# Normed transpositions for the first token tiles, and first operands made per contraction tile, in a one-core hybrid encoder kernel

## The chip, the cores and the metric

The kernel runs on one core of one Trainium2 chip. The metric is the device time of one execution in microseconds. Engines are named as in the profile: PE is TensorE, DVE is VectorE, ACT is ScalarE, POOL is GpSimd, SP is the engine that issues most DMAs.

## The reference, cut to what matters

One layer of an encoder over 1088 tokens (1024 of a prompt and 64 new ones) of width 1024. The change sits in its first two lines.

```python
h = rms_norm(x, ln_mix_g)      # x / sqrt(mean(x*x) + eps) * ln_mix_g
proj = h @ w_in                # 1024 -> 5632 columns: u, v_g, q, k, v, gates
...                            # gMLP, windowed attention, gates, w_o
x = x + f                      # f: conv FFN: w_up, depthwise conv, gelu, w_down
y = rms_norm(x, ln_final_g)
```

## The kernel before

**Pairs and products.** All large products have the weights' 128 output channels by 1088 tokens as result, and are made two column blocks of weights at a time, a *pair* p. Tokens are cut in two halves of 544, the 8 contraction tiles of 128 into even and odd ones (4 each, KP = 4). A plain pair (0 and 1 are plain) has 8 products k = 0 to 7, each 4 contraction tiles j of 6 matmuls: the two fp32 operands are each split into a high part and a rest (`w_hi`, `w_lo`, `op_hi`, `op_lo`), three passes by two column blocks of 272. Other pairs have seven products with sums of quadrants as operands.

**Operands.** `hi_f` and `lo_f` hold the normed input in fp32. For pair 0 operand 0 is the first half of the tokens with even contraction tiles (`hi_f3`), operand 1 the first half with odd ones (`hi_f5`), operands 7 and 6 are the second half (`lo_f4`, `hi_f4`). ACT rounds an operand to `op_hi` (L1235), DVE subtracts to get `op_lo` (L1647), each in one instruction of 4 times 544 columns. The same for the weights: ACT L1201, DVE L1608, 512 columns each. DVE then makes sums of operands (L1655, L1693, L1658) for the seven-product pairs, and ACT rounds the first of them, `op_hi3`, which waits for L1655.

**The norm.** There are 9 tiles of tokens n (the last has 64 rows); SPLIT = 4, so tile 4 lies across both halves. SP loads them to `xt`. For each, ACT squares and sums rows (`square_x`, L1242), POOL makes the factors 1/sqrt(mean + eps) (`rstd`, L1082 and L1085), PE transposes eight 128x128 blocks to PSUM (`transpose_x`, L2234), ACT copies them to SBUF (`x_tile`, L1192), PE spreads the factors over partitions by one product (`spread_rstd`, L2243), and DVE multiplies block by gain by factor into the operands (its own `x_tile`, L1600), 8 instructions of 128 columns a tile. The copies `xts` are also stored to DRAM by SP (`store_xt`), for the residual much later.

**Order.** Every engine's program is written out by hand and runs in that order; an engine that waits at a semaphore holds everything behind it. Tiles 0 to 5 are normed ahead of the first product. Tiles 6, 7 and 8 are transposed between contraction tiles of products 0 and 1 (`beside_first(k, j)` on PE, called behind product k, tile j). PSUM: `reg[0]`, `reg[1]`, `reg[2]` of two banks each hold products and `side` (banks 6 and 7) everything else.

Of the kernel before, what the change touches and what calls it, by code (L numbers as in the profile page):

```python
# [7 lines left out]
ALU = mybir.AluOpType  # L8
# [127 lines left out]

PAIR_TICKS = 4 * NPROD
# [53 lines left out]
OP_ORDER = [[(n, "w") for n in (0, 1, 7, 6, 3, 2, 5, 4)]]  # L191
# [9 lines left out]
PART = {"w": slice(0, KP), "a": slice(0, KP - 1), "b": slice(KP - 1, KP)}  # L201
# [69 lines left out]
def program(nc, x_prompt, x_sample, cache_k, cache_v, cache_conv, ln_mix_g, w_in, ln_v_g, ln_v_b, w_s, b_s,  # L271
# [3 lines left out]
    with ExitStack() as ctx:  # L275
# [15 lines left out]
        def put(reg, name, shape, dt=F32, at=0):  # L291
# [119 lines left out]

        bank = [ps[:, i] for i in range(4)]
# [20 lines left out]
        s_tab = sem("s_tab")  # L433
# [227 lines left out]
        def _(sp):  # L661

            def load_x(n):
                if n >= XT:
                    sp.wait_ge(s_xt_p, n - XT + 1)
                    sp.wait_ge(s_sq, n - XT + 1)
                sp.dma_start(xt[0:rows_of(n), n % XT, :], token_rows(n)).then_inc(s_x_in[n % XT], 16)

# [12 lines left out]
            for n in range(NT):  # L681
# [386 lines left out]
        def _(pool):  # L1068
# [9 lines left out]
            def rstd(n, table, sums, factors):  # L1078
# [6 lines left out]
                pool.tensor_tensor(table[0:r, 2, n:n + 1], table[0:r, 1, n:n + 1], half_neg[0:r, :],  # L1085
                                   ALU.pow).then_inc(s_rstd, 1)

            for n in range(NT):
                rstd(n, stat, 0, 0)

            def distances():
                pool.wait_ge(s_hf, NT + 1)
# [1487 lines left out]
```

## Time and profile before

| | |
|---|---|
| time, median of 3 runs | 1651.01 us (1650.73 to 1655.04) |
| the profiled execution's own time | 1649.72 us |
| its span | 1647.9 us |
| mean granted TensorE clock | 0.994 of full |
| PE busy | 1614.5 us, 98% of the span |
| DVE, ACT, POOL busy | 1152.0, 706.7, 71.7 us |
| instructions | 32421 |

The profile is of one execution. Its span is the part between the first and the last instruction; its own time is 1.8 us longer. Busy time is counted from instructions' starts and ends, matmul ends are modelled, and starts of successive matmuls tell the pace better than their durations do.

### The profile page before, as it was taken

What the parts mean: (1) busy time and instruction counts of PE and PEld (TensorE: products, weight loads), DVE (VectorE), ACT (ScalarE), POOL (GpSimd) and SP (SyncE); (2) the same over time, 40 slices, a digit from 0 to 9 for tenths busy, and PEclk for the clock granted to TensorE, in tenths of its full rate; (3) what the DMA queues carried; (4) which work ended last, traced back from release to release, by engine and by line L of the source; (5) the groups of instructions that cost most, each with busy time, mean ns of one, the idle gap of its engine ahead of it and who ended that gap; (6) DMA issues with size and microseconds to landing.
All of it is one profiled execution on the core that took longest, in us unless ns stands there. A gap on an engine that the chain in (4) does not pass through costs nothing. (4 is left out here: it accounts for less than half of the span.)

```text
span 1647.9 us, 32421 instructions
## 1 busy us (share of the span) xinstructions
PE 1614.5 (98%) x12886; PEld 1574.7 (96%) x12886; DVE 1152.0 (70%) x2078; ACT 706.7 (43%) x1292; POOL 71.7 (4%) x141
## 2 busy tenths in 40 slices
PE   6999999999999999999999999999999999999998
PEld 6999999999999999999999999999999999999997
DVE  6566565656658868696525888888888776767566
ACT  7344444444444336364434534444333334343312
POOL 2000000000000000001112100000000000000001
PEclk8999999999999999999999999999999999999999
DMA  7444434343437864757743233333333427363122
GB/s 248 151 150 118 133 107 137 102 138 100 119 111 204 242 215 161 246 161 169 166 135 99 59 115 97 107 106 106 106 106 107 131 72 266 120 241 105 69 78 110
DMA packets 272472, 227.03 MB, mean 138 GB/s; under 512 B 43335, under 2 KB 223363, under 8 KB 272323
## 3 DMA queue, kind: packets, MB, share of 16 engines
q1 hardware_dynamic: 138750, 154.36, 28.2%
q10 hardware_dynamic: 131269, 66.15, 14.3%
q0 software_dynamic: 2304, 4.46, 1.7%
q8 instruction: 103, 1.69, 0.4%
q14 instruction: 46, 0.38, 0.1%
HBM read 150.56 MB, written 74.36 MB: 136 GB/s over the span
## 5 line engine op out<-in xcount | busy, mean ns | idle before, releaser
L2296 PE MATMUL ps<-op_hi,w_hi 128*128 128x272 f32 x3672 | 775.6, 292 | 15.5 <-issue 5.6
L2296 PE MATMUL ps<-op_hi,w_lo 128*128 128x272 f32 x3672 | 760.6, 289 | 0.0
L2296 PE MATMUL ps<-op_lo,w_hi 128*128 128x272 f32 x3672 | 758.6, 288 | 0.0
L2296 PEld LDWEIGHTS ps<-op_hi,w_hi 128*128 128x128 f32 x3672 | 576.1, 189 | 32.7 <-issue 30.2
L2296 PEld LDWEIGHTS ps<-op_lo,w_hi 128*128 128x128 f32 x3672 | 578.0, 189 | 0.0
L2296 PEld LDWEIGHTS ps<-op_hi,w_lo 128*128 128x128 f32 x3672 | 575.0, 189 | 0.0
L1608 DVE TENSOR_TENSOR w_lo<-raw,w_hi 128x512 fp32r<-128x512 f32 x256 | 173.7, 698 | 157.2 <-ACT w_hi L1201 157.2
L1201 ACT ACTIVATE w_hi<-raw 128x512 fp32r<-128x512 f32 x256 | 153.7, 625 | 134.1 <-PE ps L2296 90.1
L1280 ACT ACTIVATE u<-ps 128x544 f32<-128x544 f32 x106 | 66.2, 624 | 237.6 <-PE ps L2296 237.4
L1201 ACT ACTIVATE w_hi<-w_f 128x512 fp32r<-128x512 f32 x159 | 95.3, 625 | 39.6 <-DVE w_f L1628 30.4
L1608 DVE TENSOR_TENSOR w_lo<-w_f,w_hi 128x512 fp32r<-128x512 f32 x159 | 104.8, 683 | 3.9 <-ACT w_hi L1201 3.4
L1305 ACT ACTIVATE sc_sb<-sc_sb,att_stat 128x192 f32<-128x192 f32 (+2 forms) x136 | 59.1, 435 | 92.6 <-DVE att_stat L1874 92.5
L1647 DVE TENSOR_TENSOR op_lo<-lo_f,op_hi 128x2176 fp32r<-128x2176 f32 (+2 forms) x32 | 75.1, 2348 | 21.9 <-ACT op_hi L1235 21.8
L1235 ACT ACTIVATE op_hi<-lo_f 128x2176 fp32r<-128x2176 f32 (+2 forms) x32 | 62.1, 1959 | 48.2 <-DMA lo_f<-g_spill 28.3
L1753 DVE TENSOR_TENSOR quad<-u,ps 128x544 f32<-128x544 f32 x69 | 49.3, 715 | 31.0 <-ACT u L1280 19.6
L1280 ACT ACTIVATE m1c<-ps 128x544 f32<-128x544 f32 x53 | 32.6, 615 | 59.3 <-PE ps L2296 41.7
L1647 DVE TENSOR_TENSOR op_lo<-r,op_hi 128x2176 fp32r<-128x2176 f32 (+2 forms) x25 | 42.8, 1723 | 14.9 <-ACT op_hi L1235 14.7
L1968 DVE SCALAR_TENSOR_TENSOR conv<-a_ext,conv_w,conv 128x1090 f32<-128x1090 f32 x22 | 29.8, 1354 | 29.0 <-ACT conv L1428 29.0
L1428 ACT ACTIVATE conv<-a_ext,consts,conv_w 128x1090 f32<-128x1090 f32 x22 | 28.6, 1301 | 46.7 <-issue 40.7
L1753 DVE TENSOR_TENSOR quad<-m1c,ps 128x544 f32<-128x544 f32 x23 | 16.6, 720 | 45.3 <-PE ps L2296 44.5
L1868 DVE CUSTOM_DVE_ANT_0 sc_sb<-ps,bias,sinks 128x192 f32<-128x192 f32 (+2 forms) x136 | 47.1, 401 | 0.3 <-issue 0.3
L1433 ACT ACTIVATE conv<-conv 128x1090 f32<-128x1090 f32 x22 | 24.6, 1117 | 49.2 <-DVE conv L1973 49.2
(191 smaller groups left out, 1514.1 us busy)
## 6 DMA issues: line engine op xcount, KB each, us to landing
in_spill<-quad SPq DMA_DIRECT2D x88, 272.0 KB, 2.3
raw<-in_w_up_dram ACTq DMA_DIRECT2D x44, 512.0 KB, 4.7
raw<-in_w_in_dram ACTq DMA_DIRECT2D x42, 512.0 KB, 5.4
g_spill<-value_out SPq DMA_DIRECT2D x22, 544.0 KB, 2.7
t_spill<-t_buf SPq DMA_DIRECT2D x8, 1088.0 KB, 4.3
lo_f<-g_spill SPq DMA_DIRECT2D x8, 1088.0 KB, 7.9
lo_f<-t_spill SPq DMA_DIRECT2D x8, 1088.0 KB, 9.3
raw<-in_w_down_dram ACTq DMA_DIRECT2D x16, 512.0 KB, 5.2
```

Of the source, the lines that this page charges most:

```text
L1201: act.activation(w_hi[n][:], weight_source(p, n), copy).then_inc(s_w_hi, 1)
L1235: act.activation(op_hi[at][:, j], operand_source(g, n)[:, j], copy).then_inc(s_op_hi, 1)
L1280: act.activation(two((m1c, u2, u3)[i][:]), reg[0][:, :, 0:HB], copy).then_inc(s_copied, 1)
L1305: act.activation(x, x, ACT.Exp, bias=a[:, 1, e:e + 1], accum_out=a[:, 3, e:e + 1])
L1428: act.activation(conv[:, 2:EXT], a_ext[:, 2:EXT], ACT.Identity, bias=b_conv_c[:, f:f + 1], scale=conv_w[:, 2, f:f + 1]).then_inc(s_c0, 1)
L1433: act.activation(conv[:, 2:EXT], conv[:, 2:EXT], ACT.Gelu_apprx_tanh).then_inc(s_gelu, 1)
L1608: dve.tensor_tensor(w_lo[n][:], weight_source(p, n), w_hi[n][:].bitcast(F32), ALU.subtract).then_inc(s_w, 1)
L1647: dve.tensor_tensor(op_lo[at][:, j], operand_source(g, n)[:, j], op_hi[at][:, j].bitcast(F32), ALU.subtract).then_inc(s_op, 1)
L1753: dve.tensor_tensor(two(out), two(first[:]), reg[region][:, :, 0:HB], op).then_inc(s_comb, 1)
L1868: last = dve.tensor_tensor_reduce(sc_sb[:, i % 2, h, columns_of(n, c)], side[:, h, columns_of(n, c)], bias[:, h, seen(n, c):SPAN], HD ** - ...
L1968: dve.scalar_tensor_tensor(cv, a_ext[:, 1:EXT - 1], conv_w[:, 1, f:f + 1], cv, ALU.mult, ALU.add).then_inc(s_c1, 1)
L2296: last = pe.matmul(out[:, h, 0:HB], (w_hi, w_lo)[a][place][:, j, :], (op_hi, op_lo)[b][at][:, j, HB * h:HB * h + HB], start=fresh and j == ...
```

## The change

Tiles 1 to 4 are no longer transposed and then scaled. POOL makes a matrix `diag[n]`, the identity times the tile's factors, and PE multiplies each block of the tile by it, which transposes and norms at once (`turn_normed`, 8 fp32 matmul calls a tile into `side`, even contraction tiles in bank 0, odd ones in bank 1). DVE applies the gains while it copies from PSUM (`x_turned`: one instruction of 4 times 128 columns for the even and one for the odd tiles). The gains come by a small DMA and transposition of their own. Tile 0 keeps the old way but is copied by DVE. Since the store for the residual still needs the plain transposes, tile 1 is also transposed ahead of the first product, and tiles 2, 3 and 4 within products 4, 5 and 6 of pair 0; the other tables follow in product 7. Tiles 5 to 8 keep the old way; 5 is normed beside product 1. Operands 0, 1, 7 and 6 of pair 0 are rounded and subtracted contraction tile by contraction tile (544 columns each), and PE waits for one tile at a time. SP holds the loads of tiles 6 to 8 until the first weights have landed. In the diff below the function `beside_first` shown whole is ACT's; the last lines are of PE's `beside_first`; the wait on `s_xts` for tiles 3 and 4 is in PE's `transpose_x`.

```diff
+TURNED = (0, 1, 5, 6, 7, 8, 2, 3, 4)
+COPIED = (5, 1, 6, 7, 8, 2, 3, 4, "tables")
+DIAG = range(1, SPLIT + 1)
...
-OP_ORDER = [[(n, "w") for n in (0, 1, 7, 6, 3, 2, 5, 4)]]
+OP_ORDER = [[(n, str(k)) for n in (0, 1, 7, 6) for k in range(KP)] + [(n, "w") for n in (3, 2, 5, 4)]]
...
+        turned_at = (reg[0], reg[1], side, side, side, reg[2], reg[2], reg[2], reg[2])
...
             for n in range(5):
                 load_x(n)
             load_weights(sp, 0)
-            for n in range(5, NT):
+            load_x(5)
+
+            sp.wait_ge(s_raw, 32)
+            for n in range(6, NT):
                 load_x(n)
...
+                if turned:
+                    last.then_inc(s_var, 1)
+                    pool.wait_ge(s_var, factors + n + 2)
+                    last = pool.tensor_tensor(diag[n][:], ident[:], table[:, 2, n:n + 1].broadcast_to([P, P]), ALU.mult)
...
-            square_x(0)
-            x_tile(0)
-            square_x(1)
...
-            for n in range(2, 6):
+            for n in range(6):
                 square_x(n)
-                x_tile(n)
             weight_hi(0, 0)
             weight_hi(0, 4)
-            operand_hi(0, 0, "w")
-            operand_hi(0, 1, "w")
+            for k in range(KP):
+                operand_hi(0, 0, str(k))
+            x_tile(5)
+            x_tile(1)
...
+            def beside_first(k, j):
+
+                if (k, j) == (3, 1):
+
+                    act.wait_ge(s_sq, NT)
+                if j == 0 and k in (3, 4):
+                    for i in range(KP):
+                        operand_hi(0, {3: 7, 4: 6}[k], str(i))
+                if (k, j) in ((4, 1), (6, 1), (7, 1)):
+                    x_tile({4: 2, 6: 3, 7: 4}[k])
+                if (k, j) == (7, 2):
+                    tables()
...
+            def x_turned(n, half, k):
+
+                dve.wait_ge(s_rb_p, spread_count(n, k))
...
+                dve.tensor_tensor(place_of(half, k)[:, :, t0:t0 + b - a], side[:, k].rearrange("p (i t) -> p i t", i=KP)[:, :, a:b], gain,
+                                  ALU.mult).then_inc(s_hf, 1)
...
+                if n in (3, 4):
+                    pe.wait_ge(s_xts, COPIED.index(n - 1) + 1)
...
+            def turn_normed(n):
+
+                pe.wait_ge(s_x_in[n], 16)
+                pe.wait_ge(s_rstd, n + 1)
+                for k in range(2):
+                    if n > 1:
+                        pe.wait_ge(s_hf, normed_count(n - 1, 0, k))
+                    for i in range(KP):
+                        kt = 2 * i + k
+                        last = pe.matmul(side[:, k, i * P:i * P + P], xt[:, n, kt * P:kt * P + P], diag[n][:], start=True, stop=True)
+                    last.then_inc(s_rb_p, 1)
...
+                if p == 0 and j:
+                    pe.wait_ge(s_op, op_count(0, operand, str(j)))
...
-                if (k, j) in ((0, 0), (0, 3), (1, 1)):
-                    transpose_x({(0, 0): 6, (0, 3): 7, (1, 1): 8}[k, j])
-                if (k, j) in ((0, 2), (1, 0), (1, 3)):
-                    spread_rstd({(0, 2): 6, (1, 0): 7, (1, 3): 8}[k, j])
+                if (k, j) in ((1, 0), (1, 2), (3, 0), (3, 2)):
+                    spread_rstd({(1, 0): 5, (1, 2): 6, (3, 0): 7, (3, 2): 8}[k, j])
+                if (k, j) in ((1, 0), (2, 1), (3, 0), (4, 2), (5, 2), (6, 2)):
+                    transpose_x({(1, 0): 6, (2, 1): 7, (3, 0): 8, (4, 2): 2, (5, 2): 3, (6, 2): 4}[k, j])
```

Three places show how instructions move. The first is PE's program from its start to the first product (`xt_113` is the input, `stat_110` the factors). Before:

```order
L2234 MATMUL ps<-ident_106,xt_113 128x128 [waits s_x_in1]
L2234 MATMUL ps<-ident_106,xt_113 128x128 x7
L2308 MATMUL ps<-ident_106,tab_rows_123 128x110 [waits s_tab_in]
L2309 MATMUL ps<-ident_106,tab_rows_123 128x54
L2243 MATMUL ps<-ident_106,stat_110 128x128 [waits s_rstd]
L2234 MATMUL ps<-ident_106,xt_113 128x128 [waits s_tab,s_x_in2]
L2234 MATMUL ps<-ident_106,xt_113 128x128 x7
```

With the change, from the spreading of tile 0's factors:

```order
L2332 MATMUL ps<-ident_106,stat_110 128x128 [waits s_rstd]
L2321 MATMUL ps<-ident_106,xt_113 128x128 [waits s_x_in1]
L2321 MATMUL ps<-ident_106,xt_113 128x128 x7
L2344 MATMUL ps<-diag1_126,xt_113 128x128 [waits s_rstd,s_x_in1]
L2344 MATMUL ps<-diag1_126,xt_113 128x128 x7
L2344 MATMUL ps<-diag2_127,xt_113 128x128 [waits s_hf,s_rstd,s_x_in2]
L2344 MATMUL ps<-diag2_127,xt_113 128x128 x3
L2344 MATMUL ps<-diag2_127,xt_113 128x128 [waits s_hf]
L2344 MATMUL ps<-diag2_127,xt_113 128x128 x3
```

Transposes of tiles 2 to 5 with a spreading each gave way to products with the diagonals of tiles 1 to 4, four calls for each parity, and the transposition of tile 5.

The second place is ACT's program from the stores of pair 0's first quadrants to the weights of pair 1 (`quad` is a result, `lo_f3_73` the sum that DVE makes, `xts2_118` the copy of tile 2). Before:

```order
L1379 ACTIVATE quad2_104<-ps 128x544 [waits s_product]
L1235 ACTIVATE op_hi3_52<-lo_f3_73 128x2176 [waits s_op,s_t,s_hf]
L1201 ACTIVATE w_hi0_77<-raw_98 128x512 [waits s_product,s_raw]
L1201 ACTIVATE w_hi4_81<-raw_98 128x512 [waits s_product,s_raw]
L1379 ACTIVATE quad1_103<-ps 128x544 [waits s_product]
```

With the change:

```order
L1421 ACTIVATE quad2_104<-ps 128x544 [waits s_product,s_sq]
L1281 ACTIVATE op_hi6_55<-hi_f4_67 128x544 [waits s_hf] x4
L1281 ACTIVATE op_hi3_52<-lo_f3_73 128x2176 [waits s_op,s_t,s_hf]
L1231 ACTIVATE xts2_118<-ps 128x1024 [waits s_xt_p]
L1247 ACTIVATE w_hi0_77<-raw_98 128x512 [waits s_product,s_raw]
L1231 ACTIVATE xts3_119<-ps 128x1024 [waits s_xt_p]
L1247 ACTIVATE w_hi4_81<-raw_98 128x512 [waits s_product,s_raw]
L1421 ACTIVATE quad1_103<-ps 128x544 [waits s_product]
```

The copies of tiles 2 and 3 are new here, and the copy of tile 2 stands behind `op_hi3`, which waits for the sum (`s_t`).

The third place is PE's program in product 5 of pair 0, from its third contraction tile. Before:

```order
L2296 MATMUL ps<-op_hi2_51,w_hi4_81 128x272 x2
L2296 MATMUL ps<-op_lo2_58,w_hi4_81 128x272 x2
L2296 MATMUL ps<-op_hi2_51,w_lo4_88 128x272 x2
L2296 MATMUL ps<-op_hi2_51,w_hi4_81 128x272 x2
L2296 MATMUL ps<-op_lo2_58,w_hi4_81 128x272 x2
```

With the change:

```order
L2401 MATMUL ps<-op_lo2_58,w_hi4_81 128x272 x2
L2401 MATMUL ps<-op_hi2_51,w_lo4_88 128x272 x2
L2321 MATMUL ps<-ident_106,xt_113 128x128 [waits s_xts,s_x_in3]
L2321 MATMUL ps<-ident_106,xt_113 128x128 x7
L2401 MATMUL ps<-op_hi2_51,w_hi4_81 128x272 [waits s_op]
```

The transposition of tile 3 stands between two contraction tiles, and waits for ACT's copy of tile 2 (`s_xts`), because both use `side`.

## Rows read from the trace of the kernel before

**Rows 1.** The page, part 1: busy us (share of the span) xinstructions

```profile
PE 1614.5 (98%) x12886; PEld 1574.7 (96%) x12886; DVE 1152.0 (70%) x2078; ACT 706.7 (43%) x1292; POOL 71.7 (4%) x141
```

**Rows 2.** Timeline, PE: start us, us, engine line op xcount [idle before <-releaser]

```profile
4.73 3.65 PE L2234 MATMUL ps<-ident,xt 128*128 128x128 f32 x16 [4.73 <-DMA xt<-in_x_prompt_dram]
...
9.56 1.06 PE L2234 MATMUL ps<-ident,xt 128*128 128x128 f32 x8
...
23.79 0.79 PE L2296 MATMUL ps<-op_hi,w_hi 128*128 128x272 f32 x2 [5.09 <-issue]
...
54.68 0.52 PE L2296 MATMUL ps<-op_hi,w_hi 128*128 128x272 f32 x2 [0.34 <-DVE w_lo L1608]
```

**Rows 3.** Windows of the start; the last two numbers are DMA share and GB/s

```profile
0.00:9.00 9.00, 4.14 (x19) 3.61 (x19) 0.00 (x0) 4.49 (x6) 1.69 (x12) 1.00 0.79 296
9.00:12.20 3.20, 2.59 (x21) 2.19 (x20) 2.64 (x11) 3.15 (x7) 1.27 (x4) 1.00 1.15 315
12.20:13.60 1.40, 1.27 (x10) 1.12 (x10) 1.40 (x7) 1.40 (x4) 0.27 (x2) 1.00 1.11 376
...
24.00:28.00 4.00, 4.00 (x19) 4.00 (x20) 4.00 (x7) 1.46 (x3) 2.77 (x2) 0.50 0.01 2
```

**Rows 4.** Timeline of ACT, columns as in rows 2

```profile
4.96 1.06 ACT L1242 ACTIVATE x_junk<-xt 128x1024 f32<-128x1024 f32 x1
5.92 0.19 ACT L1242 ACTIVATION_READ_ACCUMULATOR x_junk<-xt 128x1 f32 x1
...
9.30 1.03 ACT L1192 ACTIVATE xts<-ps 128x1024 f32<-128x1024 f32 x1
...
17.98 1.19 ACT L1201 ACTIVATE w_hi<-raw 128x512 fp32r<-128x512 f32 x2
...
46.71 2.03 ACT L1235 ACTIVATE op_hi<-lo_f 128x2176 fp32r<-128x2176 f32 x1 [4.12 <-DVE lo_f L1655]
48.64 1.13 ACT L1201 ACTIVATE w_hi<-raw 128x512 fp32r<-128x512 f32 x2
```

**Rows 5.** Timeline of POOL

```profile
6.47 0.56 POOL L1085 TENSOR_TENSOR stat<-stat,columns 128x1 f32<-128x1 f32 x1
...
24.78 1.89 POOL L1082 TENSOR_SCALAR stat<-stat 128x1 f32<-128x1 f32 x1 [6.65 <-ACT x_junk L1242]
```

**Rows 6.** Timeline of PE at the mixing of tokens, fp32 products at full clock

```profile
511.34 1.95 PE L2430 MATMUL ps<-ws_t,gs 128*128 128x128 f32 x16
513.04 0.50 PE L2296 MATMUL ps<-op_hi,w_hi 128*128 128x272 f32 x2
```

**Rows 7.** Timeline of DVE

```profile
9.56 9.62 DVE L1600 SCALAR_TENSOR_TENSOR hi_f<-xts,consts,ps 128x128 f32<-128x128 f32 x40 [9.56 <-PE ps L2243]
...
44.21 2.42 DVE L1655 TENSOR_TENSOR lo_f<-lo_f,hi_f 128x2176 f32<-128x2176 f32 x1
...
53.94 1.89 DVE L1608 TENSOR_TENSOR w_lo<-raw,w_hi 128x512 fp32r<-128x512 f32 x3
```

**Rows 8.** Groups by form: busy us, mean ns of one | idle before

```profile
L1120 POOL TENSOR_TENSOR m1c<-m1c,u 128x544 f32<-128x544 f32 x6 | 8.4, 1396 | 43.6 <-ACT u L1411 43.6
...
L1647 DVE TENSOR_TENSOR op_lo<-r,op_hi 128x544 fp32r<-128x544 f32 x8 | 6.5, 808 | 5.4 <-ACT op_hi L1235 5.4
...
L2211 DVE TENSOR_TENSOR xy<-ps,xy 128x512 f32<-128x512 f32 x8 | 5.5, 690 | 3.9 <-PE ps L2547 3.9
```

**Rows 9.** Timeline of PE after its wait at 1400 us

```profile
1403.14 0.49 PE L2296 MATMUL ps<-op_hi,w_hi 128*128 128x272 f32 x2 [2.97 <-DVE xy L1777]
...
1405.47 0.65 PE L2296 MATMUL ps<-op_lo,w_hi 128*128 128x272 f32 x2
1405.92 0.66 PE L2296 MATMUL ps<-op_hi,w_lo 128*128 128x272 f32 x2
...
1407.99 0.41 PE L2296 MATMUL ps<-op_lo,w_hi 128*128 128x272 f32 x2
1408.24 0.41 PE L2296 MATMUL ps<-op_hi,w_lo 128*128 128x272 f32 x2
```

More of the change, by code:

```diff
@@ L133, in chunk, with normed_count, spread_count @@
     return a * P, min(b * P, T)
+TURNED = (0, 1, 5, 6, 7, 8, 2, 3, 4)
+COPIED = (5, 1, 6, 7, 8, 2, 3, 4, "tables")
+NORMED = ("gains", "copy") + tuple((n, int(n > SPLIT), k) for n in range(SPLIT) for k in range(2)) \
+    + ((SPLIT, 0, 0), (SPLIT, 0, 1), (SPLIT, 1, 0), (SPLIT, 1, 1)) + tuple((n, 1, k) for n in range(SPLIT + 1, NT) for k in range(2))
+DIAG = range(1, SPLIT + 1)
+SPREAD = tuple((n, k) for n in range(NT) for k in range(2 if n in DIAG else 1))
+def normed_count(n, half, k):
+    return NORMED.index((n, half, k)) + 1
+def spread_count(n, k=0):
+    return SPREAD.index((n, k)) + 1
 PAIR_TICKS = 4 * NPROD
@@ L410, in program @@
         pset = [ps[:, 0:3], ps[:, 3:6]]
+        turned_at = (reg[0], reg[1], side, side, side, reg[2], reg[2], reg[2], reg[2])
+        factors_at = {n: reg[2][:, 0, 0:P] if n == 0 else side[:, n % 2, 0:P] for n in range(NT) if n not in DIAG}
         bank = [ps[:, i] for i in range(4)]
@@ L432, in program @@
         s_tab_p = sem("s_tab_p")
[L433 removed]
+        s_gain_in = sem("s_gain_in")
         s_x_in = sems("s_x_in", XT)
@@ L1075, in _, with rstd @@
                                pattern=[[-1, P]], channel_multiplier=1).then_inc(s_zero, 1)
-            def rstd(n, table, sums, factors):
+            def rstd(n, table, sums, factors, turned=False):
                 r = rows_of(n)
@@ L1583, in _, with place_of @@
         def _(dve):
[L1585 to L1602 removed]
+            def place_of(half, k):
+                return ((hi_f[3], hi_f[5]), (lo_f[4], hi_f[4]))[half][k]
@@ new lines, in gains, with first_copy, x_tile @@
+            def gains():
+                dve.wait_ge(s_tab_p, 1)
+                dve.tensor_copy(mix_g, reg[2][:, 1, P:P + KT]).then_inc(s_hf, 1)
+            def first_copy():
+                dve.wait_ge(s_xt_p, 1)
+                dve.tensor_copy(xts[0][:], turned_at[0].rearrange("p b (k t) -> p (b k) t", k=4)).then_inc(s_hf, 1)
+            def x_tile(n):
+                r, half = rows_of(n), int(n > SPLIT)
+                if n:
+                    dve.wait_ge(s_xts, COPIED.index(n) + 1)
+                else:
+                    dve.wait_ge(s_hf, NORMED.index("copy") + 1)
+                dve.wait_ge(s_rb_p, spread_count(n))
+                t0 = n * P - half * QT
+                for k in range(2):
+                    for i in range(KP):
+                        last = dve.scalar_tensor_tensor(place_of(half, k)[:, i, t0:t0 + r], xts[n][:, 2 * i + k, 0:r],
+                                                        mix_g[:, 2 * i + k:2 * i + k + 1], factors_at[n][:, 0:r], ALU.mult, ALU.mult)
+                    last.then_inc(s_hf, 1)
```

192 lines of the change are left out of this document (108 added, 84 removed).

## The prediction

> **What bounds the kernel now.** The first part of the page comes first: PE is busy 98% of the span [rows 1]. So the kernel is as long as PE's work plus the times PE stands still, and a change gains only what it takes from either. The timeline of PE shows where it stands still: the first product starts at 23.79, behind 5.09 us of idle time, and pair 1 starts at 54.68 after a wait of only 0.34 us [rows 2]. Of some 33 us in which PE isn't busy (1647.9 less 1614.5) about 20 lie ahead of the first product. The windows show that PE also starts slow: 0.50 of its clock is granted from 24 to 28 us [rows 3].
>
> From pair 1 on PE goes on without a gap to speak of, so I work out when pair 1 starts with the change. The difference to 54.68 is the forecast, as long as nothing behind it depends on the start.
>
> **Up to the first product.** The input comes at DMA speed: 9 us at 296 GB/s are 2.66 MB, which is tiles 0 to 4 (2.62 MB); 3.2 us at 315 bring the first weights (1.05 MB) to about 12.2, and 1.4 at 376 bring tile 5 to 13.6 [rows 3]. ACT now only squares. A square holds it for 1.15 us (4.96 to the end of 5.92 + 0.19), so tile n's sum is there at 6.1 + 1.15n up to tile 4 at 10.7, and tile 5, which waits for its data, at 14.75 [rows 4]. POOL ends a factor 0.9 us after the sum (6.11 to 7.03 for tile 0) [rows 5], and adds the diagonal. No row shows that product. 544 columns of a POOL product take 1.396 us [rows 8]; 128 of them in proportion are 0.33, and 1.4 is the upper bound. I take 0.4, by the proportion and a little for the start. Diagonals 1 to 4 are then there at about 8.7, 10.0, 11.4 and 12.7.
>
> PE transposes tile 0 and then tile 1 at the pace of the 16 transposes of before, 0.228 us each [rows 2], to about 9.1. A turn is 8 fp32 calls, 16 instructions of 128 columns. The mixing of tokens has the same form: 16 of them hold PE for 1.70 us (511.34 to 513.04) at full clock [rows 6]. Four turns are 6.8 us, to 15.9; at half clock they would be 13.6, which is the other bound. I take full clock, because before PE had gone from 0.228 to 1.06 / 8 = 0.13 us a transpose by 9.56 [rows 2], and is busier now. The diagonals are no later than PE. DVE empties a bank of 512 columns in 0.61 to 0.69 [rows 8] while PE fills the other in 0.85, so it keeps up: with its copy of tile 0 and the 8 old instructions (9.62 / 40 = 0.24 each [rows 7]) it is at 9.9 when the first bank is full.
>
> Behind tile 5's square, at 14.75, ACT rounds two weights (1.19 [rows 4]) to 15.9 and the first quarter of the operand to 16.5. DVE makes the last pieces of tile 4 (to 16.25), a weight's rest (1.89 / 3 = 0.6 [rows 7]) and the first quarter of `op_lo`. 544 columns take 0.808 us in the mean [rows 8], while a quarter of the long instruction is 0.6; I take 0.68 from start to start. **The first product starts at 17.6, 6.2 us earlier than before.**
>
> **To product 4.** From there DVE sets the pace. In order: three quarters of operand 0 (2.05), a weight (0.6), the rest of tile 4 (2 times 0.5), a weight (0.6), tile 5 (8 times 0.25 = 2.05), operand 1 (2.7), tile 6 (2.05), a weight (0.6): 29.25. PE has meanwhile done products 0 to 2 at 3.0 us each (two matmuls each 0.25 [rows 9], 24 in a product) with two transpositions, and waits for that last weight. It then does one contraction tile (0.75) and spreads tile 7's factors: 30.2. DVE norms tile 7 to 32.25; tile 8's factors come at 32.4 from PE's place behind tile 2 of product 3, and DVE is done at 34.05; the first quarter of operand 7 follows, and **product 4 starts at 34.8**.
>
> **The stall that the change makes.** Transpositions of tiles 2, 3 and 4 now share `side`, and each waits for ACT's copy of the one ahead. ACT's copy of tile 2 stands behind `op_hi3`, and that waits for DVE's sum of operands, which comes after all quarters of operands 7 and 6. Before, ACT already waited 4.12 us for this sum, but nothing of PE's stood behind it [rows 4]. Now:
> - DVE: 7 more quarters, 4.75, to 39.5, and the sum, 2.42 [rows 7], to 41.95.
> - ACT: `op_hi3` holds it for 1.93 (46.71 to 48.64) and a copy takes 1.03 [rows 4]: 44.95.
> - PE arrives at tile 3's transposition behind 7 contraction tiles (5.25) and tile 2's transposition (8 of 0.106 by rows 6, 0.85) at 40.9.
>
> PE stands still for about 4.1 us, to 45.05. Behind PE's waiting transposition is all of pair 0 that is left: 3 + 0.25 products (9 contraction tiles, 6.75), two transpositions (1.7), the tables (0.25), and 0.2 for the copy of tile 4, which ACT does only after product 6. That is 8.9 us, so pair 1 starts at 54.0 at full clock. DVE's part for pair 1 is ready earlier: its sum begins at 39.5, and the same list took from 44.21 to about 54.6 before [rows 7], so it ends at about 50.
>
> A stall of that length costs clock too. After 2.97 us of idle time at 1400 PE went from 0.25 us for two matmuls to 0.45, and back by 1407.99: about 3.4 us at that pace, 7 or 8 rows that lose 0.2 each, 1.5 us [rows 9]. After the 5.09 us at the start it ran at 0.50 for some 4.8 us and lost about 2.3 [rows 2, 3]. I take 1.9. **Pair 1 starts at 55.9, 1.2 us later than before.**
>
> In the sum: 6.2 us are gained at the first product; pair 0 loses a slow clock of 2.3 at its start, but takes on three transpositions (2.55), a spreading (0.2) and the tables (0.25), stands still some 2.4 us for DVE in products 3 and 4 and 4.1 us for ACT, and loses 1.9 to the clock. The stores of tiles 2 to 4 are late too (tile 4's at about 52). What needs their room or SP's turn behind them comes in the second half of pair 1 or later, and the products of pair 1 (8 of 3.0) hide them, so I cost them at nothing; without that cover PE would wait for the landing, a few us.
>
> The profiled execution would become 1649.7 + 1.2 = 1650.9; it lies 1.3 below the median of the runs, so the median would be **1652.2 us**.
>
> **A rule against the row.** PE's clock had risen after nothing but transposes, as said above. The Trainium skill (TensorE: Matmul & The Clock Gate, Part 4: PE-mode transpose) says that transposes don't count as activity for the clock gate. By that rule the turns would be the first work that counts, and the trace contradicts it for now, since PE's pace doubled behind 16 transposes. What it would do is the third rival below.
>
> POOL's 1.89 us for a 0.19 us kind of instruction at 24.78 [rows 5], beside a long DVE subtraction of two SBUF operands, is a warning for the diagonals, but beside DVE's work with a PSUM operand POOL took 0.56. The Trainium skill (GPSIMD Engine Reference, 8. Key points) has POOL share its SBUF interfaces with DVE when that has two SBUF inputs.
>
> **The rivals.**
> - *The stall without its price in clock.* PE's idle time is broken up or the clock holds: pair 1 at 54.0, 0.7 earlier, 1650.3 us. For it: nothing but that the granted clock falls at moments that a trace can't foretell. Chance 0.2.
> - *No stall.* ACT comes to the copy in time, and PE reaches pair 1 at 54.0 - 4.1 = 49.9, just when DVE has its weights: 4.7 us gained, 1646.3. Against it: the order on ACT is fixed, and the sum can't come before operand 6. Chance 0.08.
> - *Turns begin slow, slower by a front that is late.* If the first two turns run at half clock, everything behind moves by 3.4 us, pair 1 to 59.3: 1655.6. Chance 0.05.
> - *The whole turning is slow.* With all four turns at half clock, or a diagonal of 1.4 us held up by DVE, the first product comes up to 6.8 us later than I say, and the extra work and the stall stay: up to 1659. It decides when the first product starts behind 21.4 (3.8 later), from where the loss passes 5 us. Chance 0.08.
> - *The forecast*: 0.55, from 1650.5 to 1654. The rest, 0.04, for transfers of pairs 1 and 2 that come late.
>
> **The numbers.** 0.3% is 5 us, about what the measurement can tell. The forecast, the first rival and most of the second and third lie within: 0.85. Faster by more needs the second at its upper end and a start better than mine: 0.05. Slower: the last rival and part of the third, 0.10. For 8 times in 10 I take 1647.5 to 1655.5: it leaves out half of the second rival and the fourth.
>
> **What would show it.** The first product at 17 to 18.5 and product 4 at 34 to 36; an idle time of 3 to 5 us ahead of tile 3's transposition in product 5, put down to ACT's copy; a granted clock near 0.5 behind it; ACT idle before `op_hi3` until DVE's sum; pair 1 at 54 to 57. The forecast is wrong if PE isn't idle there, if the turns take over 2.5 us a tile, or if PE gains or loses gaps after pair 1.

## The result: 6 us slower, and the profile after

The change takes 1658.42 us in the median of 7 runs (1657.12 to 1663.4), the kernel before 1651.99 in its 7 (1649.33 to 1655.04): a ratio of 1.0043, interval 1.0032 to 1.0055. Measured once more it had 1658.38 (11 runs) beside 1653.04 (34 runs), ratio 1.0033, 1.0019 to 1.0048. The forecast was 1652.2, with a range of 1647.5 to 1655.5, so it is wrong by 6.2 us.

The page of the change, first part. PE is as busy a share as before [rows 1], but its busy time has grown by 8.3 us, about the length of the turns, which come on top of the transpositions; time at half clock counts as busy too.

```profile
PE 1622.8 (98%) x12943; PEld 1582.7 (96%) x12943; DVE 1151.8 (70%) x2062; ACT 707.6 (43%) x1304; POOL 72.6 (4%) x145
```

The timeline of PE up to pair 1 (start us, us, engine, line, operation, count, [idle before <- releaser]), to be read beside [rows 2]. L2401 are products, L2321 transpositions of x, L2344 turns by a diagonal.

```profile
4.59 1.97 PE L2321 MATMUL ps<-ident,xt 128*128 128x128 f32 x8 [1.32 <-DMA xt<-in_x_prompt_dram]
7.71 0.80 PE L2332 MATMUL ps<-ident,stat 128*128 128x128 f32 x2 [1.15 <-POOL stat L1119]
8.30 1.92 PE L2321 MATMUL ps<-ident,xt 128*128 128x128 f32 x8
10.00 9.32 PE L2344 MATMUL ps<-diag,xt 128*128 128x128 f32 x64
...
20.99 0.49 PE L2401 MATMUL ps<-op_hi,w_hi 128*128 128x272 f32 x2 [0.79 <-DVE w_lo L1681]
...
39.60 0.49 PE L2401 MATMUL ps<-op_hi,w_hi 128*128 128x272 f32 x2 [1.97 <-issue]
...
43.05 1.48 PE L2321 MATMUL ps<-ident,xt 128*128 128x128 f32 x8
...
49.60 1.06 PE L2321 MATMUL ps<-ident,xt 128*128 128x128 f32 x8 [2.08 <-ACT xts L1231]
...
55.05 1.04 PE L2321 MATMUL ps<-ident,xt 128*128 128x128 f32 x8
...
63.59 1.04 PE L2439 MATMUL ps<-ident,ws_raw 128*128 128x128 f32 x8
```

The first product starts at 20.99, which is 2.8 us earlier than before, not 6.2. Product 4 (39.60) waits 1.97 us for operand 7. Tile 3's transposition (49.60) waits 2.08 us for ACT's copy of tile 2, the stall that was foretold at 4.1. The transposition of `ws_raw`, in pair 1, is at 63.59; before it was at 57.78, 3.1 behind the pair's start at 54.68 [rows 2]. So pair 1 starts at about 60.5, 5.8 later than in this profile of before. The second profiles of both, further down, make that 4.4 in the mean.

The windows of PE at four places (busy us, instructions, granted clock, DMA share, GB/s):

```profile
10.00:12.00 2.00, 2.00 (x11) 1.00 1.20 292
14.00:16.00 2.00, 2.00 (x18) 1.00 0.80 166
42.00:44.00 2.00, 2.00 (x11) 0.51 0.00 0
52.00:54.00 2.00, 2.00 (x11) 0.50 0.75 224
```

Between 10 and 12 us PE starts 11 instructions in 2 us, from 14 on 18: its pace doubled in between, at about 13.4, though the column of the granted clock says 1.00 throughout. Behind both waits it says 0.51 and 0.50, the lower of its two levels (1.2 and 2.4 GHz). ACT around the square of tile 5 and around the copy:

```profile
14.59 1.06 ACT L1288 ACTIVATE x_junk<-xt 128x1024 f32<-128x1024 f32 x1 [2.88 <-DMA xt<-in_x_prompt_dram]
...
46.53 2.02 ACT L1281 ACTIVATE op_hi<-lo_f 128x2176 fp32r<-128x2176 f32 x1 [3.45 <-issue]
48.46 1.00 ACT L1231 ACTIVATE xts<-ps 128x1024 f32<-128x1024 f32 x1
```

`op_hi3` (2.02 us) is there ahead of the copy of tile 2 (48.46), in the order that the prediction read from the code. DVE while it takes the turned tiles from PSUM, and before product 4:

```profile
14.43 0.69 DVE L1674 TENSOR_TENSOR hi_f<-ps,consts 128x512 f32<-128x512 f32 x1 [0.20 <-PE ps L2344]
15.48 0.69 DVE L1674 TENSOR_TENSOR hi_f<-ps,consts 128x512 f32<-128x512 f32 x1 [0.36 <-PE ps L2344]
...
34.08 1.12 DVE L1664 SCALAR_TENSOR_TENSOR lo_f<-xts,consts,ps 128x128 f32<-128x128 f32 x4 [1.40 <-PE ps L2332]
...
37.20 0.86 DVE L1664 SCALAR_TENSOR_TENSOR lo_f<-xts,consts,ps 128x64 f32<-128x64 f32 x4 [0.96 <-PE ps L2332]
...
38.78 2.63 DVE L1720 TENSOR_TENSOR op_lo<-lo_f,op_hi 128x544 fp32r<-128x544 f32 x4
```

Each half of a turned tile takes 1.0 us from start to start, of which DVE works 0.69 and then waits for PE. Later it waits 1.40 and 0.96 us for PE's spreading of tiles 7 and 8 (L2332); operand 7's quarters start at 38.78 and product 4 follows 0.82 us behind. POOL's diagonal and one of its slow instructions:

```profile
8.97 0.40 POOL L1123 TENSOR_TENSOR diag<-ident,stat 128x128 f32<-128x128 f32 x1
...
28.66 1.41 POOL L1116 TENSOR_SCALAR stat<-stat 128x1 f32<-128x1 f32 x1 [3.05 <-ACT x_junk L1288]
```

### The profile page after: what moved, and what is told of

Read it like the earlier page. It is cut to its first block, busy times and chain, and to the rows that moved or that the text cites. A ratio compares the mean times of both kernels' runs of the same rounds, so it can differ in the third digit from the quotient of the medians.

```text
span 1656.6 us, 32537 instructions
## 1 busy us (share of the span) xinstructions
PE 1622.8 (98%) x12943; PEld 1582.7 (96%) x12943; DVE 1151.8 (70%) x2062; ACT 707.6 (43%) x1304; POOL 72.6 (4%) x145
## 4 chain that ended last, share of the span: by engine, by line
PE 61%; issue 11%; DVE 4%; DMA 3%; ACT 1%; POOL 1%; ACTq 0%; POOLq 0%; DVEq 0%; SPq 0%
PE ps L2401 52%; PE ps L2623 3%; DMA lo_f<-g_spill 1%; PE ps L2660 1%; PE ps L2543 1%; DVE op_lo L1720 1%; PE ps L2485 1%; DMA r<-m_spill 1%; DMA r<-o_spill 1%; DMA raw<-in_w_down_dram 1%; POOL r L1173 1%; DVE w_lo L1681 1%; PE ps L2515 1%; PE ps L2533 0%; PE ps L2520 0%
## 5 line engine op out<-in xcount | busy, mean ns | idle before, releaser
L2401 PE MATMUL ps<-op_hi,w_hi 128*128 128x272 f32 x3672 | 775.6, 292 | 15.1 <-DVE xy L1860 4.0
L2401 PE MATMUL ps<-op_hi,w_lo 128*128 128x272 f32 x3672 | 760.7, 289 | 0.0
L2401 PE MATMUL ps<-op_lo,w_hi 128*128 128x272 f32 x3672 | 758.6, 288 | 0.0
L2401 PEld LDWEIGHTS ps<-op_hi,w_hi 128*128 128x128 f32 x3672 | 575.6, 188 | 33.0 <-issue 29.3
L2401 PEld LDWEIGHTS ps<-op_lo,w_hi 128*128 128x128 f32 x3672 | 577.9, 189 | 0.0
L2401 PEld LDWEIGHTS ps<-op_hi,w_lo 128*128 128x128 f32 x3672 | 574.9, 189 | 0.0
L1281 ACT ACTIVATE op_hi<-r 128x2176 fp32r<-128x2176 f32 (+2 forms) x25 | 35.6, 1434 | 21.8 <-PE ps L2401 13.6
```

The costliest lines, as they stand in the source:

```text
L1281: act.activation(op_hi[at][:, j], operand_source(g, n)[:, j], copy).then_inc(s_op_hi, 1)
L2401: last = pe.matmul(out[:, h, 0:HB], (w_hi, w_lo)[a][place][:, j, :], (op_hi, op_lo)[b][at][:, j, HB * h:HB * h + HB], start=fresh and j == ...
```

## The experiments

The table has the places that the experiments speak of: starts on PE in us in one profiled execution each (in brackets the idle time before), the first product, product 4, tile 3's transposition and the `ws_raw` transposition (3.1 behind pair 1's start). "Rest" is from there to the first product that waits for `d_lo`, near 1560. The last columns are the median of the runs and the ratio to the kernel before, measured beside it on the same chip, with its interval; the kernel before had 1652.41 there beside e1, e2, e6 and e7, 1652.66 beside e4, e5 and e8, and 1653.04 beside the rest.

| kernel | product 0 | product 4 | tile 3 | ws_raw | rest | median | ratio |
|---|---|---|---|---|---|---|---|
| before | 23.79 | | | 57.78 | 1500.6 | 1651.99 | |
| before, second profile | 25.13 | | | 59.62 | 1500.4 | 1652.66 | |
| change | 20.99 | 39.60 (1.97) | 49.60 (2.08) | 63.59 | 1503.2 | 1658.42 | 1.0043 |
| change, second profile | 19.89 | 38.51 (1.99) | 48.51 (2.23) | 62.52 | 1505.6 | 1658.38 | 1.0033 [1.0019, 1.0048] |
| e1 copy ahead | 20.99 | 39.59 (1.97) | 47.36 (0) | 59.79 | 1504.1 | 1656.42 | 1.0026 [1.0014, 1.0038] |
| e2 late spread | 19.53 | 38.12 (1.96) | 48.11 (2.03) | 60.56 | 1503.0 | 1659.77 | 1.0043 [1.0027, 1.006] |
| e6 early spreads | 19.74 | 36.81 (0.71) | 46.80 (3.62) | 60.77 | 1507.3 | 1659.03 | 1.0037 [1.0025, 1.0049] |
| e5 filler | 21.34 | 39.95 (1.98) | 49.95 (filled) | 62.41 | 1504.6 | 1657.8 | 1.0028 [1.0017, 1.0039] |
| e4 parts only | 21.38 | | | 57.39 | 1502.3 | 1652.57 | 1.0 [0.9991, 1.0009] |
| e7 all three | 19.47 | 36.53 (0.69) | 42.75 (0) | 55.62 | 1502.4 | 1651.8 | 0.9999 [0.9988, 1.0011] |
| e7 again | 19.16 | 37.07 (1.54) | 43.27 (0) | 56.16 | 1502.2 | 1652.41 | 1.0002 [0.9989, 1.0014] |
| e8 four banks | 20.39 | 37.45 (0.69) | 43.66 (0) | 56.55 | 1511.1 | 1653.7 | 1.0009 [0.9997, 1.002] |
| e9 warm | 18.50 | 36.28 (1.41) | 42.49 (0) | 55.37 | 1504.6 | 1651.93 | 0.9991 [0.9977, 1.0004] |
| e3 one block | 19.37 | 37.31 (1.59) | 42.76 (0) | 55.63 | 1506.9 | 1651.59 | 0.9993 [0.9981, 1.0006] |

**e1: the copy of tile 2 ahead of `op_hi3` on ACT.**

```diff
-                if (k, j) in ((4, 1), (6, 1), (7, 1)):
+                if (k, j) in ((4, 0), (6, 1), (7, 1)):
                     x_tile({4: 2, 6: 3, 7: 4}[k])
```

> The change with ACT's copy of tile 2 moved ahead of its rounding of op_hi3. Theory (PE stands still at tile 3's transposition because that copy stands behind op_hi3): the 2.1 us wait there and the 1.4 us of slow clock behind it go, pair 1 starts at 57.0 instead of 60.5, about 1655 us. Rival (the loss is PE's added work, and the wait hides other lateness): another wait takes its place, at most 0.5 us gained, about 1658 us.

```profile
47.36 1.04 PE L2321 MATMUL ps<-ident,xt 128*128 128x128 f32 x8
...
51.24 1.04 PE L2321 MATMUL ps<-ident,xt 128*128 128x128 f32 x8
```

The stall at tile 3 is gone, and the slow clock behind it: tiles 3 and 4 are 3.88 us apart, in the change 5.45. Product 4's wait is untouched. Pair 1 starts 3.8 us earlier, of which 2.2 is the wait and 1.6 the clock. The median is 2.0 below the change, less than the trace gives.

**e2: the spreading of tile 0's factors behind the transposition of tile 1.**

```diff
             transpose_x(0)
-            spread_rstd(0)
             transpose_x(1)
+            spread_rstd(0)
```

> The change with tile 0's factors spread behind tile 1's transposition instead of ahead of it, so that PE transposes two tiles without a pause. Theory (the first turn ran at half pace because PE paused 1.15 us before its clock had risen): the first turn takes 1.7 instead of 3.4 us, the first product starts at about 18.7 instead of 21.0, about 1656 us. Rival (transpositions don't raise the clock, only the turns do): the turn stays slow, the first product starts at 20.3 or later, about 1658 us.

```profile
4.52 3.67 PE L2321 MATMUL ps<-ident,xt 128*128 128x128 f32 x16 [1.18 <-DMA xt<-in_x_prompt_dram]
...
9.83 8.04 PE L2344 MATMUL ps<-diag,xt 128*128 128x128 f32 x64 [1.02 <-POOL diag L1123]
...
48.11 1.07 PE L2321 MATMUL ps<-ident,xt 128*128 128x128 f32 x8 [2.03 <-ACT xts L1231]
...
52.01 1.04 PE L2321 MATMUL ps<-ident,xt 128*128 128x128 f32 x8
```

The wait of 1.15 us inside the transpositions is gone, and the turns begin at 9.83 at full pace: 7.87 us from there to tile 5's transposition, where the change took 9.16 and its second profile 8.38. The first product comes at 19.53, between the two expected. That the pause had made the turn slow is not shown: with the same edit the turns took 8.00 and 7.95 in e7 but 9.21 in e8, in part at half pace, and without it 8.18 in e6. Behind the same 2.03 us of wait at tile 3 the clock did not fall this time (tile 4's transposition follows by 3.90 us, as in e1). The median does not show the gain of 3 us in pair 1's start; its interval is wide, and the profile is of the shortest of the seven runs (1655.22).

**e6: the spreadings of tiles 7 and 8 earlier on PE.**

```diff
-                if (k, j) in ((1, 0), (1, 2), (3, 0), (3, 2)):
+                if (k, j) in ((1, 0), (1, 2), (2, 3), (3, 0)):
```

> The change with the spreads of tiles 7 and 8 one place earlier on PE, behind (2, 3) and (3, 0). Theory (DVE sets the pace up to product 4 and the sum, and stood still 1.4 and 1.0 us for these two spreads): product 4 starts at 37.2 instead of 39.6, DVE's sum 2.4 us earlier, pair 1 at 58.1, about 1656 us. Rival (PE's own work sets the pace): under 0.5 us gained, 1658 us.

```profile
36.81 0.49 PE L2401 MATMUL ps<-op_hi,w_hi 128*128 128x272 f32 x2 [0.71 <-issue]
...
46.80 1.06 PE L2321 MATMUL ps<-ident,xt 128*128 128x128 f32 x8 [3.62 <-ACT xts L1231]
```

From the first product to product 4 it is 17.07 us, in the change 18.61: DVE's waits for the spreadings were 1.5 us of product 4's lateness. ACT's stall at tile 3 grows to 3.62 us, since PE comes sooner to it, and the slow clock stays behind it (tile 4 follows by 5.44 us). Counted from the first product pair 1 starts 1.6 us earlier, not 2.4, and the median, 1659.03, shows no gain.

**e7: all three edits.**

> The three edits together. Theory: the first product at 18.7, no wait ahead of product 4 and tile 3's transposition, full clock through pair 0, pair 1 at about 50.5, that is 1648.5 us, 3.5 below the kernel before. Rival (the added fp32 products and transpositions cost more than the earlier start is worth): pair 1 no earlier than 54.7, 1652 us or more.

> The kernel with all three edits once more, beside the change itself in the same call. Theory (what follows pair 1 costs the same but for steps of 0.5 to 3 us at later waits that differ from one execution to the next): the first product at 19.5 when PE's pace has doubled by 10 us, and near 21 when it doubles at 13 to 14; a median 6 us below the change and within 1.5 us of the kernel before. Rival (it is faster than before by the 3 us that pair 1 starts earlier): a median of 1649.5.

```profile
36.53 0.49 PE L2401 MATMUL ps<-op_hi,w_hi 128*128 128x272 f32 x2 [0.69 <-issue]
...
42.75 1.04 PE L2321 MATMUL ps<-ident,xt 128*128 128x128 f32 x8
...
47.05 1.06 PE L2321 MATMUL ps<-ident,xt 128*128 128x128 f32 x8 [0.26 <-ACT xts L1231]
```

From the first product to `ws_raw` it takes 36.15 and 37.00 us, in the change 42.60 and 42.63. Pair 1 starts 2.2 us earlier than in the shorter profile of before, but in neither measurement does the median leave that of the kernel before. So these waits and the slow clock behind them are about the change's loss, and without them it is a draw, not the gain of some 3 us that I expected.

**e5: transpositions of the identity while PE waits for ACT.**

```diff
+                if (k, j) == (5, 2):
+                    pe.wait_ge(s_comb, comb_count(0, Q21))
+                    for i in range(18):
+                        pe.transpose(reg[1][:, i % 2, 0:P], ident[:], ident[:])
```

> The changed kernel with 18 transpositions of the identity in the 2.1 us in which PE stood still ahead of tile 3's transposition, so that PE stays busy and its wait for ACT stays. Theory (the standstill lowers the clock, also one of 2 us): the products behind tile 3 run at 0.25 us for two, not at 0.45 for 3.1 us, and pair 1 starts 1.4 us earlier, near 59.1; the median 1.4 below the change. Rival (transpositions count as idle for the clock): the clock drops there as before or earlier, pair 1 at 60.5 or later. A clock that stays with no gain of time would say that the end of pair 0 waits for DVE or ACT.

```profile
47.76 2.13 PE L2433 MATMUL ps<-ident 128*128 128x128 f32 x18
49.95 1.07 PE L2321 MATMUL ps<-ident,xt 128*128 128x128 f32 x8
...
53.87 1.04 PE L2321 MATMUL ps<-ident,xt 128*128 128x128 f32 x8
```

The clock stays: tile 4 follows tile 3 by 3.92 us, where the two profiles of the change have 5.45 and 5.47. So the slow clock behind the stall is worth 1.5 us, apart from the stall. Counted from the first product pair 1 starts 1.5 earlier; the median, 1657.8, is 0.6 below the change and not 1.4. That the filler held the clock is likely but rests on one profile, since the clock also held behind 2.03 us of idle time in e2. The rule weighed in the prediction (the Trainium skill, TensorE: Matmul & The Clock Gate, Part 4: PE-mode transpose) fits neither this nor e9 and the second profile of before, where PE's pace doubled among the first 16 transpositions of x (2.60 and 3.31 us for them, against 3.65 at half pace), with nothing but transpositions ahead.

**e4: operands by contraction tile alone, in the kernel before.** The edit is that of `OP_ORDER`, `PART`, the loops over `operand_hi` and `operand_lo` of operands 0, 1, 7 and 6, and PE's wait for one contraction tile; the norm stays as it was.

> The kernel before with one part of the change alone: operands 0, 1, 7 and 6 of the first generation are made and waited for by contraction tile, the turning stays as it was. Theory (the parts are worth something only until DVE, whose work is the same, ends it): the first product waits for a quarter of op_hi0 and a quarter of op_lo0, so it starts near 20.6 instead of 23.79, product 4 near 38.9, and pair 1 at 53.8 instead of 54.68; median 0.9 us below the kernel before. Rival (the parts are all of what the first products need, and PE runs through): pair 1 at 51.5 and a median 3 us below. Other rival (hidden): pair 1 within 0.3 of 54.7 and the same time.

```profile
21.38 0.79 PE L2303 MATMUL ps<-op_hi,w_hi 128*128 128x272 f32 x2 [2.19 <-DVE w_lo L1610]
```

The first product comes at 21.38, 2.4 us before the earlier of the two profiles of before and 0.4 to 1.5 behind the change. The parts alone thus bring most of what the change gains there. But pair 1 comes at 54.3, 0.4 us before the earlier profile of before, and the time is that of before. Between the two PE now waits 1.6 us for tile 6's factors and 0.7 for ACT, where before it waited 0.3. That fits a pair 0 whose end is set by the lists of the other engines; it wasn't tested apart.

**e8: four banks for the turns, on top of e7.**

```diff
+        turn_at = lambda n: reg[0] if n % 2 else side
...
-                    if n > 1:
-                        pe.wait_ge(s_hf, normed_count(n - 1, 0, k))
+                    if n > 2:
+                        pe.wait_ge(s_hf, normed_count(n - 2, 0, k))
+                    elif n == 1:
+                        pe.wait_ge(s_hf, NORMED.index("copy") + 1)
...
-                        last = pe.matmul(side[:, k, i * P:i * P + P], xt[:, n, kt * P:kt * P + P], diag[n][:], start=True, stop=True)
+                        last = pe.matmul(turn_at(n)[:, k, i * P:i * P + P], xt[:, n, kt * P:kt * P + P], diag[n][:], start=True, stop=True)
```

DVE's `x_turned` reads from `turn_at(n)` too.

> The kernel with all three edits (copy of tile 2 ahead, spread of tile 0 behind tile 1, early spreads) and the products with the diagonal of tiles 1 and 3 in the two banks of reg[0], those of tiles 2 and 4 in side, so that each waits for DVE's reading of two tiles before and not of the one before. Theory A (the 2.0 us a tile are a handshake over two banks between PE and DVE): the 64 instructions take 6.8 to 7.0 us and not 8.2, the first product starts at 18.3 and not 19.5, pair 1 near 51.4, and the median is 1.2 below that of all three edits. Theory B (PE itself takes 0.122 us for one of these at full clock, 2.0 a tile): 8.1 us, first product at 19.4, and the same median as with all three edits.

DVE, with PE at its full pace:

```profile
14.30 0.69 DVE L1675 TENSOR_TENSOR hi_f<-ps,consts 128x512 f32<-128x512 f32 x1 [0.46 <-PE ps L2347]
15.19 0.69 DVE L1675 TENSOR_TENSOR hi_f<-ps,consts 128x512 f32<-128x512 f32 x1 [0.20 <-PE ps L2347]
```

A half of a tile takes 0.89 us and not 1.0, so the handshake over two banks is 0.2 us a tile; the rest of the 2.0 is PE. This execution ran at half pace up to 13 or 14 us, so its first product is late for another reason. Neither theory was right on the size: 1.8 a tile, not 1.7 and not 2.0.

**e9: PE kept busy ahead of the turns, on top of e8.**

```diff
+            for i in range(6):
+                pe.transpose(side[:, 0, 0:P], ident[:], ident[:])
             transpose_x(0)
             transpose_x(1)
             spread_rstd(0)
+            for i in range(6):
+                pe.transpose(side[:, 0, 0:P], ident[:], ident[:])
```

> The kernel with all three edits and four banks, and 6 transpositions of the identity ahead of tile 0's and 6 between the spread of tile 0 and the products with the diagonals, in stretches of 0.9 us in which PE stood. Theory (the half pace at which the turning ran up to 13 or 14 us in the change and in the kernel with four banks is the clock not yet risen, and standing PE delays it): full pace from the first product with a diagonal on, the 64 instructions in 7.2 us, first product of the operands at 18.3, pair 1 at 51.4, median 1 us below that with four banks. Rival (the clock rises at a moment of its own between 9 and 14 us, whatever PE does): first product anywhere from 18.3 to 20.4 and half pace in a part of the turning as before.

```profile
3.40 1.54 PE L2415 MATMUL ps<-ident 128*128 128x128 f32 x6
4.74 2.60 PE L2322 MATMUL ps<-ident,xt 128*128 128x128 f32 x16
...
9.45 7.38 PE L2347 MATMUL ps<-diag,xt 128*128 128x128 f32 x64 [0.63 <-issue]
...
36.28 0.49 PE L2404 MATMUL ps<-op_hi,w_hi 128*128 128x272 f32 x2 [1.41 <-DVE op_lo L1721]
```

Tiles 0 and 1 are transposed in 2.6 us, where e2 took 3.67 and e8 3.67, so PE's pace doubled among them; the turns take 7.22 to the transposition of tile 5, and the first product comes at 18.50, near the 18.3 expected. Pair 1 starts at 52.3, not at 51.4. The median is 1.8 us below that with four banks, but the intervals of the two ratios overlap, and it is that of e7.

Product 4 waits 1.41 us and starts only 0.25 us earlier than in e7, with a first product 0.97 earlier. The front is not the reason. ACT issues two transfers of weights ahead of `quad` and of the first quarter of operand 7, for which DVE waits. In e7 and then in e9:

```profile
33.42 1.03 ACTq L607 DMA_DIRECT2D raw<-in_w_in_dram  x2
34.50 0.62 ACT L1421 ACTIVATE quad<-ps 128x544 f32<-128x544 f32 x1 [0.49 <-issue]
```

```profile
32.45 1.76 ACTq L608 DMA_DIRECT2D raw<-in_w_in_dram  x2
34.25 0.63 ACT L1422 ACTIVATE quad<-ps 128x544 f32<-128x544 f32 x1 [1.21 <-issue]
```

The issue took 1.76 us in e9, 1.88 in e7 again and 1.91 in e3, and 1.03 to 1.05 in all other profiles of the change and its variants; why is not known. Against e7 again, with the same long issue, e9's first product is 0.66 us earlier and its product 4 and `ws_raw` 0.79: the front's gain arrives whole.

**e3: PE turns only the first block of tiles 2, 3 and 4, on top of e7.**

```diff
-                for kt in range(KT):
+                for kt in range(1 if n in (2, 3, 4) else KT):
```

> The kernel with all three edits, in which PE turns only the first of eight blocks of tiles 2, 3 and 4 beside pair 0 (it leaves out 21 of 24 transpositions, so the residual of these tiles is not right; DVE, ACT and the transfers do all their work). Theory (pair 0 is bound by PE now, and the first product's gain of 4 us was given back in part to the turning that moved into pair 0): 21 times 0.12 us, pair 1 at 50.0 and not 52.5, median 2.4 below that of all three edits. Rival (DVE's parts or ACT's copies end pair 0): pair 1 at 52.5 and waits of PE in place of the transpositions.

The output is wrong, as it must be. PE, then ACT:

```profile
47.83 0.30 PE L2321 MATMUL ps<-ident,xt 128*128 128x128 f32 x1 [1.79 <-ACT xts L1231]
```

```profile
44.23 2.03 ACT L1281 ACTIVATE op_hi<-lo_f 128x2176 fp32r<-128x2176 f32 x1 [2.53 <-issue]
46.16 0.61 ACT L1247 ACTIVATE w_hi<-raw 128x512 fp32r<-128x512 f32 x1
46.68 1.00 ACT L1231 ACTIVATE xts<-ps 128x1024 f32<-128x1024 f32 x1
```

The rival won, for the larger part. With 21 transpositions fewer `ws_raw` comes at 55.63, and in e7's two profiles at 55.62 and 56.16; counted from product 4 it is 18.3 us against 19.1, a gain of 0.8 where 2.3 were left out (0.77 in each of three stretches). The other part of PE's free time reappears as a wait of 1.79 us at tile 4, where e7 has 0.26, for ACT's copy of tile 3 (46.68), which stands behind `op_hi3` and a weight. At 1651.59 the time is that of e7. So it isn't mainly the moved transpositions on PE that ate the earlier first product, but the chain from DVE's operands over its sum to `op_hi3`, which has next to no slack once the waits of PE are gone.

**The change and the kernel before once more.**

> The change once more. Theory: as in its first profile, product 4 after a wait of 2.0 us, tile 3's transposition after one of 2.1, both with the clock at half behind them, pair 1 between 59 and 60.5, and a median of 1658, 5 to 7 us above the kernel before. Rival (the first seven runs were long ones): a median of 1655.

> The kernel before once more, for a second profile: which later stages differ from one execution to the next. Theory (the execution first profiled was a short one of a spread of some microseconds): the first 89 us agree within 0.3 us, with pair 1 at 54.7, and the rest is 1 to 3 us longer by 1,640 us, in steps at waits for transfers. Rival (the later growth of the offset is an effect of the change): this profile agrees with the first within 0.5 us up to the end.

The second profile of the change repeats all its waits, at 1658.38 in the median. The kernel before started its first product at 25.13 the second time. PE's pace had doubled by 8 us there, but PE then waited 1.75 us for the rows of the tables, and from about 10.8 to 14 us its granted clock was 0.50. Pair 1 came 1.8 us later, 1.3 by the first product and 0.5 by a longer stretch at 0.50 behind it (to about 31.1, against 28.7), against what I expected of its first 89 us. Behind it the two profiles of before agree within 0.2 us over 1500.

PE's waits between 100 and 800 us (line, waited for, us in total, times, longest), before and then the change's second profile (a wait of 0.4 us for `pt_mid`, in both, is left out):

```profile
PE ps L2296 <- DVE w_lo L1608: 0.5, 1, 0.5
```

```profile
PE ps L2401 <- DVE r L1836: 1.6, 1, 1.6
PE ps L2401 <- DVE quad L1836: 1.2, 2, 0.9
PE ps L2401 <- DVE w_lo L1681: 0.9, 1, 0.9
PE ps L2485 <- ACT o_sb L1370: 0.6, 1, 0.6
```

## Why the prediction was wrong

The sum was to be +1.2 us at pair 1 and nothing behind it. Measured in the profiled executions it is +5.8 at pair 1 and +2.9 behind it; in the means of two profiles of each kernel +4.4 and +3.9; in the medians of all runs 5.3 to 6.4 for both together.

- **The first product (17.6 predicted, 20.99 and 19.89 measured): the step that failed.** "I take full clock" and 1.7 us a turn were both too good. The turns began at 10.00, not at 9.1: ACT's squares started 0.6 us later, behind the issue of the gains' own small DMA (0.58 us), and the spreading of tile 0, which waited for its factors, stood inside the transpositions. The turns took 9.16 us and not 6.8. 1.07 of it is there at full pace (e2's 7.87: 1.8 a tile of PE by e8 and e9, and 0.2 of handshake over two banks), 1.3 is half pace up to 13.4. From the pace at 9.56 in the profile of before I had taken that the clock is up by then; from one execution to the next PE's pace doubled between 6 us (e9) and 14 us (e5), and part of the turns ran at half pace in 6 of 11 profiles. In e9, with PE kept busy from 3.40 on, it doubled earliest; as the moment differs by itself (13.4 and 11 in the two profiles of the change), one profile doesn't show that the filler did it.
- **To product 4 (17.2 us predicted from the first product, 18.6 measured).** DVE was rightly named as the pace-setter. The spreadings on PE, at which I let DVE wait 0.95 and 0.15 us, made it wait 1.40 and 0.96; e6 takes 1.5 back. The waits of 0.32 us in product 3 and 1.97 ahead of product 4 are about the 2.4 foretold for both, but I gave them no price in clock. The second has one, 1.6 us (e1, with the same wait, takes 7.77 from product 4 to tile 3's transposition, e7 takes 6.22), and 1.4 in the change's second profile (3.72 to tile 2's transposition against 2.33).
- **The stall for ACT (4.1 predicted, 2.08 measured).** Right in mechanism and place, as e1 shows by removing it; half the size, because PE was 6.6 us later there than I said (47.52 against 40.9) and ACT's copy only 4.6. Of the 6.6, 3.4 come from the first product, 1.4 from the way to product 4 and 1.8 from there on, the slow clock above all. Its clock was right in kind: 1.5 by e1 and e5, in a sum where 1.9 stood for all; with product 4's it is 3.1.
- **First product to pair 1** all told: 38.3 predicted, 39.5 measured. The errors within it nearly cancel, and the front's 3.4 us carry through whole.
- **Nothing behind pair 1.** Wrong by 1.3 to 3.9 us, and not settled. From `ws_raw` to `d_lo` the change takes 1503.2 and 1505.6 us, before 1500.6 and 1500.4. By the medians the step is smaller, about 1.3: taking from 1652.4 and 1658.4 the 1.8 outside the span, the 89.5 and 89.8 behind `d_lo` and the 58.7 and 63.1 up to `ws_raw` (means of the two profiles of each) leaves 1502.4 and 1503.7. PE stands idle for 11.4 and 12.2 us of that stretch before and for 14.5 and 15.2 with the change, so the step is waits for the most part. Short ones from 100 to 800 us, on `o_sb`, `quad` and `r`, stand in profiles of the change and of its variants and not in those of before (those on `r` and `quad` in e4 too). They differ from one execution to the next, e8's profile loses most (1511.1), and what makes them I didn't find. The profiles of e7 and e9 have the step too (1502.2 to 1504.6), which fits that they are level with the kernel before though their pair 1 starts earlier; it wasn't tested apart.
- **The median.** I added 1.3 for a short profiled run; the two profiles of before, 1649.72 and 1651.39, and medians of 1652.4 to 1653.0 bear that out.
- **The rivals.** The case nearest to what happened is the third, "Turns begin slow", 1655.6, at a chance of 0.05. That its 3.4 us are just what the front lost is partly chance: half pace made 1.3 of them, the late start and the price of a turn at full pace the rest. The fourth's condition, a first product behind 21.4, was not met (20.99). That turns at half clock would be rare was the misjudgement.
- **Two slips that the sum doesn't use.** PE is busy for 10.5 us ahead of the first product before, so 13.3 of its 33 idle us lie there, not about 20. And the list that opens with "In the sum" comes to a loss of 2.9 us, not 1.2; the forecast rests on the times worked out one after the other.

## What to carry to other kernels

What the busiest engine gains or is spared is worth only what the other engines' lists let through. A gain at the front that moves DVE's list as well arrived whole at pair 1 (e9 against e7 again, 0.7 and 0.8 us). But 2.3 us of PE work less within pair 0 (e3) brought pair 1 at most 0.8, since DVE's operands and the instruction of ACT in their wake set the end of pair 0. A copy that another engine waits for must not be put behind an instruction that waits itself (e1: one line, 2 us in the median). And an estimate of a kernel's first 15 us must hold both levels of the clock open, with a wait of 2 us counted as a wait and, as a rule, 1.4 to 1.6 us of clock.

No version here beats the kernel before: e7 and e9, at 0.9999 and 0.9991, are level with it and some 6 us faster than the change.

## What the runs showed of the hardware

- PE's pace at the start was half until between 6 and 14 us, though the granted clock reads 1.00 there: count instructions in a window (11 in 2 us against 18). A fall that comes later does show in the column (0.50 from 11 to 14 us in the second profile of before).
- In pair 0, idle time of 1.96 to 2.23 us was followed by a clock of 0.50 for about 3 us in 7 of 8 cases (behind 39.60 and 49.60, in the second profile behind 38.51 and 48.51), but not at 48.11 in e2 after 2.03 us. After waits of 0.7 to 1.8 us there it held (e6, e8, e9, both profiles of e7, e3), but after 1.75 us near 9 us it fell (before, second profile). The length alone doesn't decide it: the wait near 1400 us, 2.97 us long in both profiles of before, was followed by 0.50 in the first and by 1.00 in the second.
- A POOL instruction on one column took 1.41 us at 28.66, beside DVE's subtraction of two SBUF operands, and 0.19 at 6.82. It ended 0.05 us behind the subtraction, as the same one did in e7, e7 again and e9 (1.38, 0.67 and 0.87 us long), so it seems to wait for DVE's end. The diagonals took 0.40 each, as estimated, while DVE read PSUM or waited. The Trainium skill (GPSIMD Engine Reference, 8. Key points) has POOL share SBUF interfaces with DVE when that has two SBUF inputs; this trace agrees.
